# Moving PSUM reads, key rates and an identity sum between VectorE, ScalarE and GpSimd in the recurrence of a hybrid layer

## What is computed

```python
def wkv7_scan(r, w, k, v, a, b, s0, reverse):
    def step(S, inp):
        r_t, w_t, k_t, v_t, a_t, b_t = inp
        sa = jnp.einsum('bhvk,bhk->bhv', S, a_t)
        S = S * w_t[:, :, None, :] + sa[..., :, None] * b_t[..., None, :] + v_t[..., :, None] * k_t[..., None, :]
        return S, jnp.einsum('bhvk,bhk->bhv', S, r_t)
...
    for d in range(2):
        a = to_heads(jax.nn.sigmoid(lp['rw_a0'][d] + a_lo @ lp['rw_a2'][d]))
        kd = kh * (1.0 + (a - 1.0) * k_a)
        y, s_fin = wkv7_scan(rh, decay, kd, vh, -kk, kk * a, s0[d], reverse=(d == 1))
        ys.append(y)
    o = ys[0] + ys[1]
```

## Time and profile before

| what | us |
|---|---|
| median of 3 runs | 2466.56 (2465.54 to 2466.6) |
| the profiled execution | 2462.29 |
| its span, first to last instruction | 2460.6 |
| PE busy | 2263.6 (92%) |
| DVE busy | 1551.8 (63%) |
| ACT busy | 1009.5 (41%) |
| POOL busy | 265.3 (11%) |

### The profile page before, as it was taken

The page is one execution under the profiler, slowest core; times in us unless marked ns, Lnnn a source line. Parts: engine busy times, 40 slices in busy tenths (PEclk is TensorE's granted clock), DMA queues, the critical chain, the costliest instruction groups (busy, mean ns, idle before and its releaser), DMA issues. The chain is left out here.

```text
span 2460.6 us, 66375 instructions
## 1 busy us (share of the span) xinstructions
PE 2263.6 (92%) x26630; PEld 1853.4 (75%) x26630; DVE 1551.8 (63%) x2611; ACT 1009.5 (41%) x1734; POOL 265.3 (11%) x335
## 2 busy tenths in 40 slices
PE   4999999999899999999947899999788799899998
PEld 2788878888688887888836777777657576688887
DVE  5756566666865456665635777777456676856754
ACT  5444234544532123445424555555333666411111
POOL 0000000000000000000031222222124663000000
PEclk7999999999999999999978999999978899999999
DMA  7344333333242333333330111110068523834542
GB/s 240 107 135 125 111 94 111 113 117 102 94 129 93 96 108 97 106 111 119 107 101 25 32 41 32 32 56 17 19 214 305 126 94 95 288 115 171 197 152 88
DMA packets 250306, 277.75 MB, mean 113 GB/s; under 512 B 30683, under 2 KB 174171, under 8 KB 247643
## 3 DMA queue, kind: packets, MB, share of 16 engines
q1 hardware_dynamic: 245306, 266.95, 33.9%
q10 hardware_dynamic: 4576, 8.40, 0.9%
q0 software_dynamic: 320, 0.98, 0.2%
HBM read 184.66 MB, written 91.62 MB: 112 GB/s over the span
## 5 line engine op out<-in xcount | busy, mean ns | idle before, releaser
L715 PE MATMUL proj_ps<-h_hi,w_hi 128*128 128x512 f32 x1656 | 649.5, 392 | 27.6 <-DVE h_lo L465 19.7
L716 PE MATMUL proj_ps<-h_lo,w_hi 128*128 128x512 f32 x1656 | 647.0, 391 | 0.0
L717 PE MATMUL proj_ps<-h_hi,w_lo 128*128 128x512 f32 x1656 | 646.4, 390 | 0.0
L318 ACT CAST w_hi<-w_raw 128x512 fp32r<-128x512 f32 x420 | 255.1, 621 | 694.0 <-PE proj_ps L717 353.2
L715 PEld LDWEIGHTS proj_ps<-h_hi,w_hi 128*128 128x128 f32 x1656 | 312.3, 189 | 98.2 <-issue 26.1
L717 PEld LDWEIGHTS proj_ps<-h_hi,w_lo 128*128 128x128 f32 x1656 | 312.2, 189 | 65.6
L716 PEld LDWEIGHTS proj_ps<-h_lo,w_hi 128*128 128x128 f32 x1656 | 312.4, 189 | 62.9
L482 DVE TENSOR_TENSOR w_lo<-w_raw,w_hi 128x512 fp32r<-128x512 f32 x420 | 283.2, 689 | 44.3 <-ACT w_hi L318 43.7
L498 DVE TENSOR_TENSOR z_slots<-proj_ps,x_rows 128x512 f32<-128x512 f32 x174 | 120.2, 691 | 169.9 <-PE proj_ps L717 167.9
L498 DVE TENSOR_TENSOR x_rows<-proj_ps,x_rows 128x512 f32<-128x512 f32 x116 | 80.1, 691 | 108.9 <-PE proj_ps L717 102.9
L1010 POOL MEMSET rpb_padded<- 60x127 f32 x1 | 0.2, 198 | 1261.3 <-POOLq L89 1261.3
(11 more groups left out here) (380 smaller groups left out, 4101.4 us busy)
## 6 DMA issues: line engine op xcount, KB each, us to landing
w_raw<-in_w_in SPq DMA_DIRECT2D x240, 256.0 KB, 3.0
scratch_gatesT<-z_slots SPq DMA_DIRECT2D x128, 256.0 KB, 2.7
late_rows<-scratch_gatesT SPq DMA_DIRECT2D x64, 512.0 KB, 4.4
scratch_zT<-z_slots SPq DMA_DIRECT2D x108, 256.0 KB, 2.4
ada<-in_ada_w SPq DMA_DIRECT2D x4, 2048.0 KB, 15.2
late_rows<-scratch_zT SPq DMA_DIRECT2D x4, 2048.0 KB, 12.7
late_rows<-scratch_branchT SPq DMA_DIRECT2D x16, 512.0 KB, 5.3
late_rows<-in_x SPq DMA_DIRECT2D x16, 512.0 KB, 4.9
```

The source lines that it names most:

```text
L318: A.copy(wh[:, i, :, :], raw[:, q, :, :]).then_inc(w_hi, 1)
L715: T.matmul(out, wh[:, i, k, :], hi[:, o, k, :], start=(first and k == 0), stop=False, skip_group_check=not first)
L716: T.matmul(out, wh[:, i, k, :], lo[:, o, k, :], start=False, stop=False, skip_group_check=not first)
L717: last = T.matmul(out, wl[:, i, k, :], hi[:, o, k, :], start=False, stop=(k == 3), skip_group_check=not first)
```

## The change

`key_rates` (two operations per unit) moves from ScalarE to GpSimd. ScalarE copies P out of PSUM into a new buffer `pst` and the y of both directions into `yst` and `yst2`; GpSimd adds the identity to P from there; VectorE's P additions go, its two y additions of 128x256 become one of 128x512 in the next unit, and y is stored from there. `exps` is split into `exp_up` and `exp_down`, both at other places in ScalarE's list. On PE `key_sums` moves from level 4 to level 3 and `turned(Kh)` from level 3 to level 4, and the bonus product moves behind W. On VectorE `norms` moves from level 4 to level 3, `kka` and `R` out of `hats`, and `B` and `K` change places. Lists of names (`Turns`) follow the new order. Core of the diff:

```diff
+            def y_out(n):
+                main_v.after(sp, (n + 1, 0), "y.")
+                sp.dma_start(t["yT"][0, :, :, bass.ds(n * RB, RB)].rearrange("m p t -> p m t"), yst[:]).then_inc(y_stored, 16)
...
                 for d in range(2):
                     if d and more:
                         load(n + 2)
+                    if d == 0 and not first_block(n):
+                        y_out(n - 1)
...
-                    if d:
-                        main_v.after(sp, (n, 1), "Ya1.")
-                        sp.dma_start(t["yT"][0, :, :, bass.ds(n * RB, RB)].rearrange("m p t -> p m t"), yst[:]).then_inc(y_stored, 16)
...
+            def add_identity(n, d):
+                main_a.after(pool, (n, d), "P.")
+                pool.sem_inc(pool_go, 1)
+                to = Pst[:, d, bass.ds(n * 4, 4), :, :].rearrange("p (g c) m j -> p c g m j", c=2)
+                eye = i64[:, :].rearrange("p (a b j) -> p a b j", a=1, b=1).to_broadcast([P, 2, 2, CH])
+                for c in range(2):
+                    last = nc.gpsimd.tensor_tensor(to[:, c], pst[:, c].rearrange("p g (m j) -> p g m j", m=2), eye, ALU.add)
+                return last
+
+            def key_rates(n, d):
+                prep_a.after(pool, (n, d), "ta1")
+                pool.sem_inc(pool_go, 1)
+                for m in range(2):
+                    last = nc.gpsimd.tensor_scalar(uu[:, m, :], aa[:, m, :], hka[:, m:m + 1], oka[:, m:m + 1], ALU.mult, ALU.add)
+                prep_g.done(last, d, "u")
...
                 main_g.done(nc.gpsimd.tensor_copy(lora[:], lora_of[:, d, :]), d, "lora.")
+                key_rates(*nxt)
                 main_p.after(pool, (n, d), "G5.")
...
+            def norm_squares(n):
+                prep_p.after(dve, (n, 0), "ks")
+                prep_v.done(V.tensor_scalar(nx[:], ps[:, 4, 0:8], 1e-24, None, ALU.max), 0, "nx")
+
             def norms(n):
                 own = lambda ins, name: prep_v.own(dve, (n, 0), ins, name)
                 i32 = mybir.dt.int32
-                prep_p.after(dve, (n, 0), "ks")
-                own(V.tensor_scalar(nx[:], ps[:, 4, 0:8], 1e-24, None, ALU.max), "nx")
...
+            def norm_rows(n):
                 prep_v.done(V.tensor_copy(rx[:], ny[:].rearrange("p (k o) -> p k o", o=1).to_broadcast([P, 8, CH])), 0, "rx")
 
             def rates(n, d):
-                prep_a.after(dve, (n, d), "u1")
+                prep_g.after(dve, (n, d), "u")
                 prep_v.done(V.tensor_tensor(kd[:, d], uu[:], zf[:, 2:4, :], ALU.mult), d, "kd")
 
...
+            def key_rate_hat(n, d):
+                prep_a.after(dve, (n, d), "ta1")
+                prep_v.done(V.scalar_tensor_tensor(kka[:], aa[:], 1.0, kk[:], ALU.add, ALU.mult), d, f"kka{d}")
+
+            def query_hat(n, d):
+                prep_a.after(dve, (n, d), "EI")
+                if not (first_block(n) and d == 0):
+                    main_g.after(dve, (n, d), "R.", back=1)
+                prep_v.done(V.tensor_tensor(chunks(AR[:, 1, :, :]), chunks(zf[:, 0:2, :]), padded(d, 1 - d), ALU.mult), d, "R")
+
             def hats(n, d):
                 done = lambda ins, name: prep_v.done(ins, d, name)
-                if d == 0:
+                if d:
+                    query_hat(n, d)
+                else:
                     prep_p.after(dve, (n, 0), "rnT")
                     done(V.tensor_tensor(kk[:], kkr[:], ps[:, 7, :].rearrange("p (m t) -> p m t", m=2), ALU.mult), "kk")
-                prep_a.after(dve, (n, d), "tot")
+                    prep_v.after(dve, (n, 0), "kk")
+                    key_rate_hat(n, d)
                 if not (first_block(n) and d == 0):
-                    main_g.after(dve, (n, d), "R.", back=1)
-                done(V.tensor_tensor(chunks(AR[:, 1, :, :]), chunks(zf[:, 0:2, :]), padded(d, 1 - d), ALU.mult), "R")
-                if d == 0:
-                    prep_v.after(dve, (n, 0), "kk")
-                done(V.scalar_tensor_tensor(kka[:], aa[:], 1.0, kk[:], ALU.add, ALU.mult), "kka")
+                    main_p.after(dve, (n, d), "A.", back=1)
                 done(V.scalar_tensor_tensor(chunks(AR[:, 0, :, :]), chunks(kk[:]), -1.0, padded(d, d), ALU.mult, ALU.mult), "A")
+                prep_v.after(dve, (n, d), f"kka{d}")
+                prep_a.after(dve, (n, d), "EN")
+                done(V.scalar_tensor_tensor(Bh[:], kka[:], 0.5, EN[:], ALU.mult, ALU.mult), "B")
                 prep_v.after(dve, (n, d), "kd")
                 done(V.tensor_tensor(Kh[:], kd[:, d], EN[:], ALU.mult), "K")
-                prep_v.after(dve, (n, d), "kka")
-                done(V.scalar_tensor_tensor(Bh[:], kka[:], 0.5, EN[:], ALU.mult, ALU.mult), "B")
...
             def prologue():
                 mix(0, (6, 2, 3, 0, 1, 4, 5))
                 key_squares(0)
+                norm_squares(0)
                 decay(0, 0)
                 norms(0)
+                norm_rows(0)
                 rates(0, 0)
+                query_hat(0, 0)
                 hats(0, 0)
...
             def last_products(n, d, done):
-                main_p.after(dve, (n, d), "PQ.")
+                main_a.after(dve, (n, d), "P.")
                 prep_a.after(dve, (n, d), "tot")
                 for c in range(2):
                     pq = ps[:, c, :].rearrange("p (g q m j) -> p g q m j", g=2, q=2, m=2)
                     to = lambda st: st[:, d, bass.ds(n * 4, 4), :, :].rearrange("p (g c) m j -> p g c m j", c=2)[:, :, c, :, :]
                     tt = tot[:, d, bass.ds(n * 4, 4), :].rearrange("p (g c) (m o) -> p g c m o", c=2, o=1)[:, :, c, :, :]
-                    eye = i64[:, :].rearrange("p (a b j) -> p a b j", a=1, b=1).to_broadcast([P, 2, 2, CH])
-                    done(V.tensor_tensor(to(Pst), pq[:, :, 0, :, :], eye, ALU.add), f"P{c}.")
                     done(V.tensor_tensor(to(Qst), pq[:, :, 1, :, :], tt.to_broadcast([P, 2, 2, CH]), ALU.mult), f"Q{c}.")
...
+                done(V.tensor_tensor(yst[:], yst[:], yst2[:], ALU.add), "y.")
...
                                              ps[:, 6:8, :].rearrange("p q (k t) -> p (q k) t", t=2 * CH), strict_of(d), ALU.mult), "MK.")
                         if nxt and d:
                             mix(nxt[0], (2, 3, 0))
+                    if v == 2 and d == 0:
+                        add_y(n - 1, done)
                     if v == 2 and nxt and d:
                         mix(nxt[0], (1, 4, 5))
                         key_squares(nxt[0])
                     if v == 3 and nxt:
+                        if d:
+                            norm_squares(nxt[0])
                         decay(*nxt)
+                        if d:
+                            norms(nxt[0])
+                        else:
+                            key_rate_hat(*nxt)
                     if v == 4 and nxt:
                         if d:
-                            norms(nxt[0])
+                            norm_rows(nxt[0])
                         rates(*nxt)
                         if d == 0:
                             bonus_rows(n)
+                        else:
+                            query_hat(*nxt)
                 if nxt:
                     hats(*nxt)
...
                 for c in range(2):
-
-                    main_a.after(dve, (n, 0), f"Y{c}.")
-                    if d:
-                        y = yst[:].rearrange("p m (g c t) -> p c g m t", g=2, c=2)[:, c]
-                        done(V.tensor_tensor(y, ps[:, 4 + c, 256:512].rearrange("p (g m t) -> p g m t", g=2, m=2), y, ALU.add), f"Ya{c}.")
+                    main_a.after(dve, (n, d), f"Y{c}.")
...
-            def key_rates(n, d):
-                prep_a.after(act, (n, d), "ta1")
-                for m in range(2):
-                    prep_a.done(A.activation(uu[:, m, :], aa[:, m, :], ACT.Identity, scale=hka[:, m:m + 1], bias=oka[:, m:m + 1]), d, f"u{m}")
-
-            def exps(n, d):
+            def exp_up(n, d):
+                prep_v.after(act, (n, d), "inc" if d else "L")
+                prep_a.done(A.activation(padded(d, 1 - d), chunks((inc if d else L)[:]), ACT.Exp, scale=0.5 * DECAY), d, "EI")
+
+            def exp_down(n, d):
                 own = lambda ins, name: prep_a.done(ins, d, name)
-                prep_v.after(act, (n, d), "inc" if d else "L")
-                run = chunks((inc if d else L)[:])
-                own(A.activation(padded(d, 1 - d), run, ACT.Exp, scale=0.5 * DECAY), "EI")
...
                 factor(X[:], "X3.", 4)
                 factor(Z[:], "Z3.", 0)
-                rows(Kt, "Kt.", "K.")
                 if d == 0:
                     main_p.after(act, (n, d), "V.")
                     own(A.copy(flat(Vt[:]), ps[:, 6, :]), "V.")
                 if nxt:
-                    key_rates(*nxt)
+                    exp_up(*nxt)
+                    if d:
+                        exp_down(*nxt)
+                rows(Kt, "Kt.", "K.")
                 factor(X[:], "X4.", 4)
                 factor(Z[:], "Z4.", 0)
```

(59 more changed lines are left out.)

29 lines of the change are left out of this document (19 added, 10 removed).

## The result

The changed kernel takes 2475.4 us in the median of six runs (2473.57 to 2479.85) against 2466.57 of six runs of the kernel before beside them (2462.32 to 2467.01). The ratio is 1.0039, with a 95% interval of 1.0027 to 1.0051: slower by 0.39%, or 8.8 us, where 7.1 us and 0.29% were forecast. The forecast range of 2460 to 2481 us holds the median.

A forecast was written before the change was run, and what follows sets the result against it. TensorE was taken as the bound. +0.52 us per d = 0 unit and +0.18 per d = 1 unit made 5.6 over eight pairs; with one-time costs 7.1, so 2466.56 became 2473.7 us, range 2460 to 2481.

The forecast's parts named there:

- case (1): Local part of the recurrence: as computed, both delays on the path, 2469 to 2481 us; chance 0.50.
- `At.` wait: d = 0 units: `exp_down` delays ScalarE's copy of `A`, so the norm transposes wait 0.54 us more.
- Exchange of levels, d = 1: Levels 3 and 4: G4's mask waits for the norm operations, X4 +0.66 us; unit +0.18 in sum.
- Free as well: GpSimd's key rates: at most twice 1.34 us, done by 13.5 in d = 0, before `kd` at 13.9.
- Exchange of levels, d = 0, +0.23: Levels 3 and 4: `key_sums` delays X3, mask latency keeps level 4 from giving it back; X4 +0.23 us.
- Tail, -0.24 per unit: Z5 to first scores: W follows Z5 sooner, the bonus product behind W hides the hats' wait; 0.24 us gained.
- P and y, a gain of 0.34 in d = 1 and 0.14 in d = 0: VectorE loses P operations: G2 starts 0.34 us sooner in d = 1, `w_lora` moves forward 0.14 in d = 0.
- One-time costs, 1.5: Outside the repeated pairs: unit (0, 0) 0.5 us, prologue 0.5, end of the recurrence 0.5.
- Nothing here is to be had from the clock.: 16 middle units: TensorE's granted clock is already 1.00, the 2.4 GHz level, so no gain there.
- (2): Whole loop: freed engines win, level exchange and norms cost nothing, a pair gains 1.3 us; 2458 us, chance 0.17.
- (3): Local part: only one of the two delays shows, `exp_down` finding a gap; 2469 us, within 0.2%, chance 0.28.
- (4): GpSimd's key rates come late, over 4.4 us in d = 0; 1 us further gives 17, 2490 us; chance 0.05.

The follow-up runs named there:

- c2: c1 with `exp_down` put back ahead of ScalarE's copy of `A` in d = 0 units; 2460.88 us, 0.9987 of the kernel before.
- c1: a3 with `kka` and `R` back in `hats`; 2453.41 us, 0.9957 of the kernel before.
- a1: The changed kernel with ScalarE's copy of `A` ahead of `exp_down` again in d = 0 units; 2477.49 us, 1.0051 of the kernel before.
- after: The changed kernel itself, with the whole change, against the kernel before; 2475.4 us, ratio 1.0039.
- a4: The changed kernel with GpSimd's key rates held until behind VectorE's norm chain in d = 1 units; 2479.03 us, 1.0059 of the kernel before.
- c3: c1 with the exchange of levels 3 and 4 put back as in the change; 2473.75 us, 1.0044 of the kernel before.
- a2: The changed kernel with the exchange of levels 3 and 4 undone on TensorE and VectorE; 2483.72 us, 1.0080 of the kernel before.
- c4: c1 with the bonus product ahead of W again, as in the kernel before; 2451.65 us, 0.9942 of the kernel before.
- b1: The kernel before with only P and y through ScalarE, identity on GpSimd and the single y sum; 2457.02 us, ratio 0.9963.
- d1: The kernel before with two unread VectorE additions ahead of the mask of G5 in d = 1 units; 2476.9 us, ratio 1.0041.
- a3: The changed kernel with the edits of a1 and a2 together; 2474.86 us, 1.0039 of the kernel before.
- c5: c1 with `R` put back ahead of the mask of G5 in d = 1 units; 2469.99 us, 1.0024 of the kernel before.
- b2: The kernel before with only the key rates moved to GpSimd; 2464.79 us, ratio 0.9995.

## Why the prediction was right

Its sign was right and the total came near, and case (1) came in: both delays are on the path. The nearness of the total is in part luck. A pair of units was forecast to cost 0.70 us and costs 1.2, so the loop costs 9.6 us at full clock where 5.6 was taken, and other terms cancel the difference. The steps in order:

- **`At.` wait, +0.54 per d = 0 unit.** Measured 0.54; `norm_columns` at 17.24 where 17.17 was forecast. c2 against c1 gives 0.62, a1 against after 0.57. Right.
- **Exchange of levels, d = 1.** X3 at 11.21 (forecast 11.25), G4 at 13.39 (13.43). X4 came at 15.96, forecast 15.65. The mechanism, the mask behind the norm chain, is the one in DVE's rows. The 0.31 was missing: the running sum takes 1.31 for 1.23 and a small operation 0.35 for 0.17 beside GpSimd's key rates, and there are gaps. a4 gave 0.27 of it back. The step "Free as well" held for GpSimd's own time and not for what it does to VectorE. The Trainium skill ("GPSIMD Engine Reference", § 8 Key points) states contention between GpSimd and VectorE instructions with two SBUF inputs. The forecast weighed this for GpSimd alone. The trace agrees with it in both directions: the pair of key rates takes 2.24 us beside the sum and 1.09 where it stands behind it, and the sum itself grows by 0.08. First scores at 22.70 (22.36), unit 27.31 (27.00), so +0.49 in place of +0.18.
- **Exchange of levels, d = 0, +0.23.** X4 at 14.06, as forecast. c3 against c1 gives 0.33. In the changed kernel `kka` ahead of G4's mask gives the same delay by itself, as a2 showed: it was one delay with two causes, and the forecast named one.
- **Tail, -0.24 per unit.** Wrong. In the changed kernel the first scores of d = 0 come 3.58 us after Z5, before 3.66, so 0.08 of the 0.24 is there: from W to the bonus product it is 1.04 us where 0.89 was taken. And the place behind W doesn't earn even that. c4 against c1: the bonus product behind W costs 0.40 in d = 0 and nothing in d = 1. The forecast was that it would "hide the hats' last 0.87 us"; but with `kka`, `R` and P's additions out of the way the last hat of d = 0 is ready 2.0 us before the first scores, nothing is left to hide, and the 0.80 us wait ahead of W stays open. That the product would cost as much in the changed kernel was not tried. First scores at 21.37 (21.18), unit 25.98 (25.82), so +0.70 in place of +0.52.
- **P and y, a gain of 0.34 in d = 1 and 0.14 in d = 0.** b1: 0.43 and 0.13. Right.
- **One-time costs, 1.5.** The start of the stage to the first G1 took 50.70 us and before 47.68, so 3.0 where 0.5 (0 to 2.0) was taken, past the bound. 2.59 of it is one gap of VectorE before `rx`, put down to issue. The same gap, 2.50 and 2.78 us, stands in a1 and a4 and in none of the others; its cause stays open. Unit (0, 0) took 1.15 us more, where 0.5 (0 to 0.6) was taken: in after, the clock is still at 0.50 until about 1318 us, 4 us into the unit, and before it was back at 1.00 ahead of G1. The end was +0.6 (forecast 0.5). Behind the recurrence's local part the program was 2.5 us shorter and ahead of it 0.9 longer, also unexplained.
- **"Nothing here is to be had from the clock."** Nothing to win, but there was something to lose. Before, the 16 middle units have no wait over 0.9 us and no drop. The change puts a wait of 1.15 to 1.30 into the d = 1 units. All eight kernels with repeated waits of 1.0 to 2.0 us in these units have four to seven drops, and the six kernels without have none. In the profiled execution of after they cost about 5 us (434.7 us to the written-out unit against 420.35 before, less 9.6). How many stand in the median run wasn't measured: the loop's 9.6 and one-time costs already exceed the 8.8. So the sum came out near partly by terms that cancel.

What causes a drop is shown only so far. In d1, a2, a3 and c5 it comes within 2.5 us behind the start of Z5 that ends the wait. In after, a1, a4 and c3 a drop that follows a long wait comes 20 us or more behind it, in a later unit, amid dense work: in unit (3, 0) PE had waited no more than 0.33 us since G1, when this window of after fell.

```profile
1490.00:1494.00 4.00, 4.00 (x100) 3.66 (x100) 2.56 (x4) 1.49 (x3) 2.35 (x3) 0.57 0.00 0
```

Not every long wait is followed by one. The last drop of a1 comes some 155 us behind the last of its three waits over 1 us, and a4's first drop, at 1353 us, has only waits of unit (0, 0) ahead of it (up to 1.55 us at 1331.76); single waits of 1.4 to 1.9 us stand in that unit in all six kernels without drops too. Which wait leads to which drop stays open; that waits and drops come together is what fourteen profiles show. The same profiles are parted as well by the length of a pair at full clock: 52.1 us or less in the six without drops, 52.4 or more in the eight with them. No run has the added idle time of PE in many short pieces, so whether a long wait is needed or idle time as such is enough is untested.

That a1 and a4, with shorter units than after, have no lower median fits their seven drops to its four, and one more number: the mean granted clock of the whole launch lies between 0.958 and 0.962 in the six runs of a1 and between 0.961 and 0.965 in those of a4, against 0.964 to 0.968 in those of after. These means don't say where in the launch the clock was low, and in c2, whose profile has no drop in the loop, they too run from 0.963 (2468.11 us) to 0.974 (2454.40 us).

Of the rivals, (2) gave the wrong kernel: the freed engines do win, 0.43% to 0.58%, 11 to 14 us, but only once `exp_down`, the exchange and the two hats are out of the way (c1 and c4). (3) is refuted: the wait for `At.` stands in the rows of after, and in c2 and in c3 each delay shows alone. (4) didn't come: 2.04 us a unit.

## What to carry to other kernels

Relief of an engine and reordering of its list are two changes. Here the relief changed the time by -0.4% (b1), and the order that came with it by +0.8% (after against b1), the drops of the clock included. When an operation is placed ahead of another that the bound engine waits for, price it there even if it takes only 0.7 us. Beyond its length, count a repeated wait of a microsecond on TensorE as a risk of lowered clock in the units around it. Undo steps from both sides, since one removed from the changed kernel can be covered by one that stayed.

## What the hardware showed unexpectedly

- TensorE at half clock in the midst of a loop in which it is busy 89% of the time; a single drop costs 0.5 to 1.7 us of a unit, least where it falls ahead of the long wait and fills it, as in unit (5, 1) of after. Matmul groups then take up to 2.07 for 1.12 us.
- A VectorE operation of 128x512 with two SBUF inputs grows beside GpSimd. The y sum took 1.22 us beside the end of `neighbours`, in after as in b1; `kd` took 1.10 in a3 beside the reset of MB, and `kka` 0.78 in after beside the key rates. Without GpSimd beside them each takes 0.68 or 0.69. The masks, which read PSUM, kept 0.69 beside it. The y sum and its neighbour in after, DVE and then POOL:

```profile
1484.79 1.22 DVE L1255 TENSOR_TENSOR y_stage<-y_stage,y_stage_back 128x512 f32<-128x512 f32 x1
```

```profile
1482.29 3.17 POOL L1013 TENSOR_TENSOR neighbours<-z_halo 128x1792 f32<-128x1792 f32 x1
```

- GpSimd's pair of key rates took 1.09 us in unit (2, 1) of a4 and b2, where it stands behind the running sum, 2.24 in d = 1 of after, beside it, and 1.95 in d = 0 of a4, beside other operations of 512 elements.
